# Ones multiplied on TensorE during two waits: in the delta rule and at the end of the mLSTM

## What is computed

```
# mLSTM, per head and token t:
m_t = max(a_inter, max(dmat));  s_qk = (q k^T) * exp(dmat - m_t)
num = w_inter * (q C) + s_qk v; den = w_inter * (q n) + sum(s_qk)
h = num / max(|den|, exp(-m_t));  out = head_rms(h) * sigmoid(o);  y = out @ w_out

# gated delta rule, per head and chunk:
a_mat = strict(b * (k k^T) * decay) + I        # lower triangular
u = solve(a_mat, b * v) - solve(a_mat, b * exp(gam) * k) S
o = (q * exp(gam)) S + ((q k^T) * decay) u
S = exp(g_last) S + k_dec^T u
```

## Time and profile before

| what | value |
|---|---|
| median of 3 runs | 2870.57 us (2869.45 to 2872.04) |
| profiled execution, its own time | 2872.99 us |
| its span | 2871.0 us |
| TensorE busy | 2738.6 us, 95% |
| mean granted clock of TensorE | 0.965 of full speed |

### The profile page before, as it was taken

The page is one execution under the profiler, slowest core; times in us unless marked ns, Lnnn a source line. Parts: engine busy times, 40 slices in busy tenths (PEclk is TensorE's granted clock), DMA queues, the critical chain, the costliest instruction groups (busy, mean ns, idle before and its releaser), DMA issues.

```text
span 2871.0 us, 49901 instructions
## 1 busy us (share of the span) xinstructions
PE 2738.6 (95%) x21498; PEld 2625.3 (91%) x21498; DVE 1302.4 (45%) x2082; ACT 893.4 (31%) x1125; POOL 193.6 (7%) x169
## 2 busy tenths in 40 slices
PE   7999999998979999999999999998998889999999
PEld 7999999877876999999999999998987876999998
DVE  5444234234574444432444424777334573444422
ACT  4332222233323333322222222543323232333322
POOL 2000000011110100000000000001311000100000
PEclk9999999997999999999999999999978989999999
DMA  4333334122483233332333332223213472333331
GB/s 120 93 90 104 93 90 104 45 60 67 132 275 121 73 89 93 92 101 80 88 91 92 103 89 70 74 63 88 45 52 103 145 238 96 89 90 93 99 100 51
DMA packets 472628, 278.58 MB, mean 97 GB/s; under 512 B 24821, under 2 KB 460790, under 8 KB 472459
## 3 DMA queue, kind: packets, MB, share of 16 engines
q1 hardware_dynamic: 449720, 230.83, 28.4%
q0 software_dynamic: 8704, 33.56, 3.3%
q10 hardware_dynamic: 14078, 12.35, 1.4%
HBM read 259.21 MB, written 17.69 MB: 96 GB/s over the span
## 4 chain that ended last, share of the span: by engine, by line
PE 86%; DVE 5%; ACT 3%; issue 3%; DMA 1%; POOL 0%; ACTq 0%; SPq 0%; DVEq 0%; POOLq 0%
PE ACC L429 24%; PE ACC L431 24%; PE ACC L430 24%; PE ACC L1115 2%; PE M L2119 1%; ACT w_hi L512 1%; PE ACC L2119 1%; DVE w_lo L518 1%; PE M L1449 1%; PE M L1474 1%; DVE cache L1211 1%; PE M L2258 1%; PE M L2196 1%; DMA raw<-in_xa_w_k 1%; PE M L1519 1%
## 5 line engine op out<-in xcount | busy, mean ns | idle before, releaser
L429 PE MATMUL ACC<-xg_hi,w_hi 128*128 128x260 f32 x3968 | 1132.6, 285 | 11.6 <-DVE w_lo L890 7.6
L431 PE MATMUL ACC<-xg_hi,w_lo 128*128 128x260 f32 x3968 | 1126.6, 284 | 0.0
L430 PE MATMUL ACC<-xg_lo,w_hi 128*128 128x260 f32 x3968 | 1123.2, 283 | 0.0
L518 DVE TENSOR_TENSOR w_lo<-raw,w_hi 128x1024 fp32r<-128x1024 f32 (+1 forms) x326 | 421.9, 1294 | 1060.4 <-ACT w_hi L512 1054.5
L429 PEld LDWEIGHTS ACC<-xg_hi,w_hi 128*128 128x128 f32 x3968 | 753.3, 190 | 13.4 <-issue 8.6
L430 PEld LDWEIGHTS ACC<-xg_lo,w_hi 128*128 128x128 f32 x3968 | 752.6, 190 | 0.0
L431 PEld LDWEIGHTS ACC<-xg_hi,w_lo 128*128 128x128 f32 x3968 | 752.3, 190 | 0.0
L512 ACT ACTIVATE w_hi<-raw 128x1024 fp32r<-128x1024 f32 (+1 forms) x326 | 363.6, 1115 | 1234.4 <-PE ACC L431 1223.6
L430 PE MATMUL ACC<-hid_lo,w_hi 128*128 128x260 f32 x1408 | 398.3, 283 | 0.0
L431 PE MATMUL ACC<-hid_hi,w_lo 128*128 128x260 f32 x1408 | 397.6, 282 | 0.0
L429 PE MATMUL ACC<-hid_hi,w_hi 128*128 128x260 f32 x1408 | 397.4, 282 | 0.0
(11 more groups left out here) (549 smaller groups left out, 3307.7 us busy)
## 6 DMA issues: line engine op xcount, KB each, us to landing
raw<-in_ffn_w_gate SPq DMA_DIRECT2D x88, 512.0 KB, 3.8
raw<-in_ffn_w_up SPq DMA_DIRECT2D x88, 512.0 KB, 3.8
raw<-in_ffn_w_down SPq DMA_DIRECT2D x64, 704.0 KB, 4.5
cache<-in_cache_mem_k POOLq DMA_DIRECT2D x16, 1024.0 KB, 7.2
cache<-in_cache_mem_v POOLq DMA_DIRECT2D x16, 1024.0 KB, 6.7
raw<-in_gd_w_in SPq DMA_DIRECT2D x32, 512.0 KB, 4.1
raw<-in_ml_w_in SPq DMA_DIRECT2D x24, 512.0 KB, 3.9
raw<-in_xa_w_q SPq DMA_DIRECT2D x16, 512.0 KB, 4.5
```

What stands on the lines that cost most here:

```text
L429: pe.matmul(out, wh, hi[:, k0 + k, m], start=begin, stop=False)
L430: pe.matmul(out, wh, lo[:, k0 + k, m], start=False, stop=False)
L431: mm = pe.matmul(out, wl, hi[:, k0 + k, m], start=False, stop=end)
L518: dve.tensor_tensor(w_lo[:, j % 2, 0:n], raw[:, (j + d) % 4, 0:n], w_hi[:, j % 2, 0:n].bitcast(F32), ALU.subtract).then_inc(w_split, 1)
```

## The change

```diff
@@ MLstm.pe
                 ml_pe.done(pe.matmul(M[:, 3, 64:128], ones[:], ml_t8[:, 8, :], start=True, stop=True), "nsq8")
+                pe.wait_ge(acc_free, ML_O.t0 + ML_O.units)
+                pe_idle(pe, 24)
                 ml_pool.wait(pe, "yl", MLH - 2)
                 ml_dve.wait(pe, "yl", MLH - 1)
@@
+        def pe_idle(pe, count):
+            for _ in range(count):
+                pe.matmul(ACC[:, 0, 0:P], ones[:], ones[:], start=True, stop=True)
@@ Gdn.pe
                 values(0)
                 keys(0)
+                pe_idle(pe, 50)
                 y5(0)
                 x5(0)
                 xt5(0)
```

## The result

The changed kernel took 2875.97 us (median of 17 runs, 2870.92 to 2882.56), the kernel before 2870.53 (17 runs, 2864.37 to 2875.71): ratio 1.0018, 95% interval [1.0009, 1.0026]. It is slower by some 5 us, where I had forecast 0.6 us less, with 2873.3 as the upper end of the range. The profiled execution took 2879.87 us with a span of 2877.9.

The account below looks back on a forecast made before the run. The prediction took TensorE, busy for 95% of the span, as the bound, with gains only at its waits or low clock. 0 for the mLSTM and -0.6 us for the delta rule took 2870.57 to 2870.0 us, range 2867.0 to 2873.3.

Parts of the forecast that it names:

- What bounds the kernel, and the waits: TensorE busy for 95% of the span; added matmuls fall into its waits of 5.6 us (mLSTM) and 15.2 us (delta rule).
- mLSTM, 0 us: At ML_OUT: the 24 matmuls delay its start by 1.9 us, and full clock saves 1.93 us, sum 0.
- the price of 0.224 us a matmul: In both places: time of one added fp32 matmul at full clock, taken from y5 and xt5, 0.224 us.
- Delta rule, -0.6 us: At y5 and x5: the clock falls again in the remaining 4.1 us wait, but lasts less long, gaining 0.6 us.
- the sum: Over both places: 0 for the mLSTM and -0.6 us for the delta rule, together -0.6 us.
- the 1.2 us sooner: At y5 and x5: low clock of about 4.1 us, the mean of seven stretches, instead of 5.3; half is gained time.
- Rival A: In the delta rule the clock holds over the remaining 4.1 us, giving -2.6 us there, 2868.0 us; chance 0.12.
- an edge somewhat above 3.13 us: For TensorE's idle gaps: the clock survived a 3.13 us wait at 1994.72, so the limit lies somewhat above the page's 3 us.
- rival B: In both places multiplying ones doesn't count as work for the clock: +8.1 us, 2878.7 us; chance 0.04.
- the clock falling at other moments in the stages behind: Behind both places: named as an example of what the prediction doesn't see, with no size of its own.
- unseen part of 0.05: Anywhere in the kernel: chance of 0.05 left for effects not seen, such as fetching 148 added pairs of instructions.
- the 19 matmuls: In the delta rule: number of the 50 at low clock at which their end passes y5's start at 2015.06.

Follow-up runs that it names:

- e1: The changed kernel with the delta rule's 50 matmuls removed, only the mLSTM's 24 left: 2867.97 us, ratio 0.9990 to the kernel before.
- c2: The delta rule's 50 matmuls alone, without the mLSTM's 24, measured again beside the whole: 2869.36 us, ratio 0.9990 to the kernel before.
- e6: The changed kernel with 48 matmuls in the mLSTM instead of 24 and none in the delta rule: 2871.31 us, ratio 1.0001.
- e2: The changed kernel with the mLSTM's 24 matmuls and their wait removed, only the delta rule's 50 left: 2868.81 us, ratio 0.9997.
- e4: The changed kernel with each added matmul cut to one column of weights and one moving column, in both places: 2867.32 us, ratio 0.9981.
- z10: The kernel before with 10 matmuls of ones inside the dense phase GD_Z, filling no wait: 2879.85 us, ratio 1.0022.
- e5: The changed kernel with 14 matmuls in the mLSTM instead of 24 and 60 in the delta rule instead of 50: 2870.79 us, ratio 0.9994.
- e3: The changed kernel without the mLSTM's 24 matmuls and with 70 in the delta rule instead of 50: 2870.96 us, ratio 1.0011.
- z15: The kernel before with 15 matmuls of ones inside the dense phase GD_Z, filling no wait: 2871.67 us, ratio 0.9992.
- a1: The changed kernel once more, word for word: 2876.71 us, ratio 1.0011 to the kernel before.
- c1: The mLSTM's 24 matmuls alone, without the delta rule's 50, measured again beside the whole: 2866.38 us, ratio 0.9990 to the kernel before.
- a28: The changed kernel with 28 matmuls in the mLSTM instead of 24, 50 in the delta rule as before: 2878.46 us, ratio 1.0020.
- c3: The changed kernel a third time, unedited, beside its parts: 2873.01 us, ratio 1.0005 to the kernel before.
- d2: The changed kernel a fourth time, unedited, beside the mLSTM part alone: 2876.72 us, ratio 1.0014 to the kernel before.
- d1: The mLSTM's 24 matmuls alone, a third time, beside the whole: 2867.53 us, ratio 0.9996 to the kernel before.

## Why the prediction was wrong

**What bounds the kernel, and the waits: right.** Both added bursts fell into the waits that I read.

**mLSTM, 0 us: nearly right.** Measured -0.8 us in the changed kernel's first profile, and from -0.7 to -0.9 in five others with the 24, but -0.1 in e1, where the clock came back only after 5.0 us. The place scatters by itself too: c2, with nothing added there, was 1.6 us longer than the kernel before. The last of the 24 ended 1.3 us late instead of 1.9, since the clock came back 3.6 us after they began instead of 4.4. e6 confirms the price of 0.224 us a matmul.

**Delta rule, -0.6 us: that the clock falls in the remaining wait was right, the gain wasn't.** The 50 took 11.3 us for 11.2, y5 did run at the low clock in every profile with 50, and the stretch from the copy of `W` to the second chunk's keys on VectorE was as long as before in e2 and 1.0 us shorter in the changed kernel's first profile. But that 1.0 isn't the 50's: e4, with one-column matmuls, has it as well (y5 3.57 us), and so has z10. It comes with how the executions enter the delta rule. In e2, where the 50 met the conditions of the sum, the clock came back 5.3 us after y5's start, as before, and not the 1.2 us sooner that the sum took from the mean of seven other waits. Rival A would have needed a shorter gap, which e5 made: it got its 2.6 us. Nor is there an edge somewhat above 3.13 us, as the prediction read from one wait. That wait, ahead of the transposes, is 3.14 or 3.15 us long in all 20 profiles; in 12 of them the clock stayed at 1.00 through it and the transposes, in eight it fell in the wait's last half us or among the transposes (1.97 us of transposes in the kernel before, 3.63 in c2, which has nothing added ahead of them):

```profile
2000.72 3.63 PE L2128 MATMUL M<-ident,gp 128*128 128x128 f32 x16 [3.15 <-DVE gp L701]
```


**The loss came out on rival B's side (3.6 to 5.4 us of its 8.1), but not by its mechanism.** Ones do count as work: 24 of them brought the clock back in the mLSTM, and 50 kept it at 1.00 until they ended.

**The step that failed is the sum itself, which has no term for what lies behind the two places.** It adds 0 and -0.6 and lets the rest of the kernel only shift; "the clock falling at other moments in the stages behind" stood outside it, in an unseen part of 0.05. That term isn't 0. Stage G was 268.6 to 270.9 us in the four profiles of the changed kernel against 260.6 and 260.9 in the two of the kernel before, 7.7 to 10.3 us more, and over all executions the whole came out at +3.6 us. Whether a wait costs low clock behind it, and how long, hangs on where it stands against the clock's changes, and a shift of one or two us at the start of the delta rule picks between patterns that differ by 9 us at its end.

The 20 profiles sort by y5 alone: where the clock returned 4 to 5.4 us after y5's start (y5 3.75 us, x5 2.20 to 2.85) stage G was 257.0 to 260.9 us, nine profiles; where it returned after 2.8 to 3.5 us (y5 3.37 to 3.68, x5 2.01) it was 266.0 to 270.9, nine profiles; with y5 wholly at full clock (e3, e5) 260.5 and 261.6. Within the stage the granted clock was low for 51 to 58 us in the first nine, for 75 to 92 us in the second nine. The cheapest entry for y5's own 16 records is not the cheapest for the stage. That a shift alone moves a kernel from one to the other is shown by z10 and z15.

Two slips in the prediction's figures change nothing here: the upper end of its range adds the losses of 1.8 us to the forecast of 2870.0 where they count from the kernel before (2870.57), and in rival B the 19 matmuls at the low clock take 8.4 us, not 4.

**Why it takes both parts: argued, not shown.** All four profiles of the changed kernel are dear, in two ways. (All four are of executions at 2877 us or more; none of the 27 below 2875 us was profiled, and whether stage G is dear there too isn't known.) In two (the first, and a1) the clock was already low at the transposes (3.4 to 3.6 us instead of 1.97), as in c1, c2, e4, a28 and z10. In c2 nothing is added ahead of the transposes, so there it comes from layer 0 and the phases between, and the kernel before, which has the same instructions up to there, can have it too. It would explain that kernel's executions at 2875 us and more, but none of them was profiled. In the other two (c3 and d2) the transposes took 1.97 us as in the cheap profiles, and then the store of `blk` to scratch was late. The timeline of c3:

```profile
2003.37 1.07 DVE L2540 COPY blk<-W 128x1024 f32<-128x1024 f32 x1
2004.46 0.34 SPq L1988 DMA_DIRECT2D scr_x<-blk  x1
...
2009.45 1.29 DVE L2599 TENSOR_TENSOR kdec<-M,keep 128x512 f32<-128x512 f32 x2 [5.01 <-DMA scr_x<-blk]
...
2015.93 3.62 PE L2125 MATMUL M<-Xs,rr 128*128 128x128 f32 x16 [6.05 <-DMA XTs<-scr_w]
```

and that of d1, the mLSTM part alone, on the cheap pattern:

```profile
2002.82 1.29 DVE L2598 TENSOR_TENSOR kdec<-M,keep 128x512 f32<-128x512 f32 x2 [3.09 <-DMA scr_x<-blk]
...
2009.21 3.75 PE L2125 MATMUL M<-Xs,rr 128*128 128x128 f32 x16 [15.17 <-DMA XTs<-scr_w]
```

`kdec` waits 5.0 us for the store in c3 and d2, and 3.04 to 3.14 us in the 18 other profiles. The DMA view of c3 from 2004 to 2009 us has one packet of the kind "instruction" that e2, the delta rule's part alone, doesn't have beside its store:

```profile
q1 hardware_dynamic: 304, 1.25, 65.5%
q8 instruction: 1, 0.02, 1.8%
issues: line engine op xcount, KB each, median us to landing
scr_x<-blk SPq DMA_DIRECT2D x1, 512.0 KB, 4.9
```

In e2 the same view from 1999 to 2004 us (its store is issued at 2000.78):

```profile
q1 hardware_dynamic: 296, 1.25, 66.0%
issues: line engine op xcount, KB each, median us to landing
scr_w<-W SPq DMA_DIRECT2D x1, 512.0 KB, 2.6
scr_x<-blk SPq DMA_DIRECT2D x1, 512.0 KB, 3.0
```

The packets of that kind have 16 or 8 KB in these traces; I take them for fetches of code. One of 16 KB starts 1.2 to 1.4 us after the store's issue in c3 and d2. In the 18 others none starts during the store, but for a28, where one comes in its last 0.5 us and the store still takes 3.0. My reading: with the 24 of the mLSTM in the stream the next packet falls due while the 50 run, takes one of the DMA engines for 1.45 us, and the store lands 1.9 us later. y5 is then 1.9 us late and starts against the clock as on the dear pattern (back after 3.3 us), 1.0 us net at this place and 9 us behind it. Without the 24 the packet comes before the store (at 1994.4 us in e2).

So this second way was seen only with both parts, in two of the changed kernel's four profiles and in none of the 16 others; the first way was seen with either part alone as well, and how often a kernel takes it is known only from the share of its long executions. No experiment moved the packet; that is open. Open too is which wait of layer 0 sets the first way in, and why a28 took as long in all of its 12 executions (2875.3 us and more), of which one was profiled.

## What to carry to other kernels

Filling a wait to keep TensorE's clock up is worth at most the low clock behind that wait, here 1.9 and 2.6 us; if the filling leaves a gap in front of the real work, the clock can fall all the same: it did in every profile with 50 matmuls (gaps of 2.3 to 6.1 us), and didn't with 60 (1.7 us) or 70 (0.6 us). In a kernel with many such waits, a gain of 1 us at one of them can be outweighed at the later ones, since it changes how they meet the clock. Before a small change is judged, shift the work behind it by a few amounts (5, 10, 15 matmuls), repeat the kernel before as a kernel of its own, and compare stages of equal work in several profiles, not one profile of each.

## What I had not expected of the hardware

The low clock's pattern over a stage of 260 us takes few values: stage G was 257.0 to 257.6, 260.0 to 261.6, 266.0 or 268.3 to 270.9 us in 20 profiled executions of 12 different kernels. The same wait of 3.15 us, in the same place of the program, lost the clock in eight of these profiles and kept it in 12. The kernel before itself spreads over 22 us (2863.8 to 2885.4, 192 executions) without any edit. And a single 16 KB packet of instructions stands beside a store of 512 KB that landed after 4.9 us instead of 3.0.
